# V's second pass with the weights' halves in spaced runs of 32 words

## What is computed

```python
u = u_emb[expert]
a = jax.nn.gelu(jnp.einsum('thkd,td->thk', u, xb), approximate=False)
coef = (g * a).astype(xb.dtype)
return jnp.einsum('thk,thkd->td', coef, v_emb[expert])
```

## Time and profile before

| | us |
|---|---|
| median of 3 runs (3255.95 to 3256.79) | 3256.68 |
| span of the profiled execution | 3254.9 |
| TensorE busy in it | 3242.3 |
| DVE busy | 2176.9 |
| ACT busy | 1675.9 |
| POOL busy | 119.5 |

### The profile page before, as it was taken

How to read it: one execution, slowest core, us unless ns; L and a number is a source line. 1 busy time by engine, 2 the same in 40 slices (tenths; PEclk the granted TensorE clock), 3 DMA queues, 4 the chain that set the end, 5 groups by cost and what they waited for, 6 DMA issues and landing times.

```text
span 3254.9 us, 60191 instructions
## 1 busy us (share of the span) xinstructions
PE 3242.3 (100%) x24752; PEld 3093.8 (95%) x24752; DVE 2176.9 (67%) x3677; ACT 1675.9 (51%) x2630; POOL 119.5 (4%) x157
## 2 busy tenths in 40 slices
PE   9999999999999999999999999999999999999998
PEld 9999999999999999999999999999999988888887
DVE  7987486666664487665765898878655555556655
ACT  5555554444444455544555444667544444455544
POOL 0001200000000100000000000222000000000000
PEclk9999999999999999999999999999999999999999
DMA  6444555555566656445656556444555555566554
GB/s 221 150 142 136 182 171 191 188 188 188 189 190 195 194 173 204 140 160 171 190 195 211 185 194 192 163 154 146 174 192 192 193 191 193 193 211 216 192 188 163
DMA packets 168801, 594.21 MB, mean 183 GB/s; under 512 B 19696, under 2 KB 21968, under 8 KB 168400
## 3 DMA queue, kind: packets, MB, share of 16 engines
q1 hardware_dynamic: 168528, 590.36, 55.4%
HBM read 584.55 MB, written 4.19 MB: 181 GB/s over the span
## 4 chain that ended last, share of the span: by engine, by line
PE 98%; DVE 1%; ACT 0%; DMA 0%; issue 0%; SPq 0%; DVEq 0%; ACTq 0%
PE ps L902 31%; PE ps L903 31%; PE ps L904 31%; PE ps L1344 2%; PE ps L957 0%; DVE wl L1437 0%; PE ps L909 0%; PE ps L929 0%; PE ps L1152 0%; DMA raw<-in_in1k 0%; PE ps L1175 0%; PE ps L1172 0%; PE ps L1358 0%; PE ps L1186 0%; PE ps L1176 0%; PE ps L1010 0%
## 5 line engine op out<-in xcount | busy, mean ns | idle before, releaser
L2201 ACT CAST wh<-raw 128x1024 fp32r<-128x1024 f32 (+2 forms) x1118 | 1159.9, 1038 | 1226.5 <-PE ps L904 1222.4
L1437 DVE TENSOR_TENSOR wl<-raw,wh 128x1024 fp32r<-128x1024 f32 (+2 forms) x1118 | 1347.9, 1207 | 502.1 <-ACT wh L2201 499.2
L902 PE MATMUL ps<-xh,wh 128*128 128x256 f32 x3088 | 863.2, 280 | 0.8 <-ACT vm L2494 0.7
L904 PE MATMUL ps<-xh,wl 128*128 128x256 f32 x3088 | 852.4, 276 | 0.0
L903 PE MATMUL ps<-xl,wh 128*128 128x256 f32 x3088 | 852.0, 276 | 0.0
L902 PE MATMUL ps<-xw,wh 128*128 128x260 f32 (+2 forms) x2096 | 595.4, 284 | 1.0 <-DVE wl L1437 0.9
L904 PE MATMUL ps<-xw,wl 128*128 128x260 f32 (+2 forms) x2096 | 590.3, 282 | 0.0
L902 PEld LDWEIGHTS ps<-xh,wh 128*128 128x128 f32 x3088 | 580.3, 188 | 5.3 <-ACT vm L2494 1.1
L903 PEld LDWEIGHTS ps<-xl,wh 128*128 128x128 f32 x3088 | 580.3, 188 | 1.6
L904 PEld LDWEIGHTS ps<-xh,wl 128*128 128x128 f32 x3088 | 579.8, 188 | 0.0
L903 PE MATMUL ps<-xw,wh 128*128 128x256 f32 (+2 forms) x1441 | 405.8, 282 | 0.0
(11 more groups left out here) (416 smaller groups left out, 4372.7 us busy)
## 6 DMA issues: line engine op xcount, KB each, us to landing
raw<-in_peer_u SPq DMA_DIRECT2D x256, 512.0 KB, 4.2
raw<-in_peer_v SPq DMA_DIRECT2D x256, 512.0 KB, 4.4
raw<-in_w_in SPq DMA_DIRECT2D x172, 512.0 KB, 3.7
raw<-in_w_up SPq DMA_DIRECT2D x82, 512.0 KB, 4.3
raw<-in_w_gate SPq DMA_DIRECT2D x80, 512.0 KB, 4.3
raw<-in_w_down SPq DMA_DIRECT2D x80, 512.0 KB, 4.1
raw<-in_w_out SPq DMA_DIRECT2D x64, 512.0 KB, 3.9
raw<-in_w_branch_a SPq DMA_DIRECT2D x16, 512.0 KB, 3.5
```

Of the source, the lines that this page charges most:

```text
L902: t.matmul(o, lh, rh, start=start, stop=False)
L904: return t.matmul(o, ll, rh, start=False, stop=stop)
L1437: v.tensor_tensor(part_at(wl, i), raw[:, i % RN, 0:cols(i)], part_at(wh, i).bitcast(F32), ALU.subtract).then_inc(lo, 1)
L2201: s.copy(part_at(wh, i), raw[:, i % RN, 0:cols(i)]).then_inc(hi, 1)
```

## The change

In the second pass of V the high and the low half of a chunk are no longer stored as 1024 contiguous words. A new array `comb` names the memory of `wh`, `wl`, `xh` and `xl` together (it begins at byte 23200 like `wh`). The function `V_part` gives a chunk's half in it: it begins 24 words (96 bytes) into `comb`, plus the slot's place, and so at a multiple of 256 bytes; of every 64 words (256 bytes) the second 32 are used (`side` 1). A half takes 8192 bytes of address and holds 4096. ACT's conversion and DVE's subtraction write it so (their count of words is the same), and the moving operand of a matmul is 16 runs of 32 words with a step of 256 bytes. Its output in PSUM stays 512 contiguous words. The three slots lie over `xh`, `xl` (two of them), and over `wh` and the front of `wl` (the third). `c_last` moves to word 4164 of `comb`, behind that third slot, and ACT's wait ahead of writing it is now for the whole first pass. All stages before the second pass, the waits of `cut`, the chunks and the order of the instructions on every engine stay as they are.

```diff
@@ -76,6 +76,7 @@
 RN, SN = 4, 3
 CH = 1024
+RUN = 32
@@ -503,6 +504,9 @@
     raw = alloc(top, "raw", [128, RN, CH])
+    comb_scope = ExitStack()
+    comb = alloc(comb_scope, "comb", [128, 2 * SN * (CH + 128) + 8832], F32R)
+    comb_scope.close()
     wh = alloc(top, "wh", [128, SN, CH + 128], F32R)
     wl = alloc(top, "wl", [128, SN, CH + 128], F32R)
@@ -613,7 +617,18 @@
-    c_last = [x[:, PAD_X[3] - 24:PAD_X[3] - 24 + S] for x in xbuf]
+    c_last = [comb[:, 4164 + S * n:4164 + S * n + S] for n in range(2)]
+
+    TOOTH = {V1 % SN: 6912, (V1 + 1) % SN: 6912 + 4 * CH, (V1 + 2) % SN: 0}
+
+    def V_part(w, i, half):
+        if i >= V1:
+            o = 24 + TOOTH[i % SN] + 2 * CH * half
+            return comb[:, o:o + 2 * CH].rearrange("p (b side k) -> p b side k", side=2, k=RUN)[:, :, 1, :]
+        return runs(w[:, i % SN, 0:CH])
+
+    def runs(a):
+        return a.rearrange("p (b k) -> p b k", k=RUN)
@@ -1374,9 +1389,9 @@
-            tk, dd = slice(128 * qt, 128 * qt + 128), slice(512 * b, 512 * b + 512)
-            return three(acc(half, qt, b)[:], coef_at(0, n)[:, tk], coef_at(1, n)[:, tk], wh[:, i % SN, dd], wl[:, i % SN, dd],
-                         j == 0, j == 127)
+            tk, dd = slice(128 * qt, 128 * qt + 128), slice(512 * b // RUN, (512 * b + 512) // RUN)
+            return three(runs(acc(half, qt, b)[:]), coef_at(0, n)[:, tk], coef_at(1, n)[:, tk], V_part(wh, i, 0)[:, dd],
+                         V_part(wl, i, 1)[:, dd], j == 0, j == 127)
@@ -1434,6 +1449,10 @@
             v.wait_ge(hi, i + 1)
+            if i >= V1:
+                v.tensor_tensor(V_part(wl, i, 1), runs(raw[:, i % RN, 0:CH]), V_part(wh, i, 0).bitcast(F32),
+                                ALU.subtract).then_inc(lo, 1)
+                return
@@ -2198,6 +2217,9 @@
                 s.wait_ge(gemm, i - SN + 1)
+            if i >= V1:
+                s.copy(V_part(wh, i, 0), runs(raw[:, i % RN, 0:CH])).then_inc(hi, 1)
+                return
@@ -2578,7 +2600,7 @@
             if n == 255:
-                s.wait_ge(gemm, AT["U", 127, 1] + 1)
+                s.wait_ge(gemm, V1)
```

## The result

The changed kernel takes 3263.19 us (median of 13 runs, 3262.61 to 3264.16), the kernel before 3256.68 in the same comparison: ratio 1.002, 95% interval 1.0013 to 1.0027. It is slower by 6.5 us, where 20.7 us less was forecast.

A forecast was written before the change was run, and what follows sets the result against it. TensorE's matmul count times start-to-start distance was taken to bound the kernel. Span 3254.9 - 22.2 (matmuls) + 1.5 (stalls) = 3234.2 us, plus 1.8 from span to median, gave 3236.0 us; range 3231 to 3262.

The forecast's parts named there:

- the two states: V's second pass: a matmul costs 544 cycles (226.7 ns) at first, 560 (233.3 ns) later, against 512 needed.
- Step 1: Second pass's 1536 matmuls: the moving operand in upper-half runs would take 216 ns each, 22.2 us less.
- the tax: Extra cycles of a float32r moving stream reading a 4-byte word every cycle: one in 16, 32 per 512 columns.
- three different places: Sign for a tax independent of address: streams beginning at three places in their 256 bytes all show 1 in 16.
- Steps 2 to 5: Second pass: conversion and subtraction cost the same, moved slots 0 us, moved last coefficients 1.5 us allowed, DMA 0 us.
- step 4: Last coefficients moved in `comb`: new wait 0 us; 1.5 us allowed for the end stall and `fin` steps with faster chunks.
- The second state: Second pass from about 3039 us: 560 cycles a matmul, begun where DVE's `fin` steps crowd its queue, never restored.
- Nothing changes: Rival for the second pass: unchanged mix, 3256.7 us, or second state throughout, 4.4 us more, 3261.1; chance 0.14.
- the tax stays: Rival for the second pass: tax remains, second state goes; all matmuls 226.7 ns, 5.8 us less, 3250.9; chance 0.16.
- The slower rival: Second pass: each jump over 128 unused bytes restarts the operand fetch; 576 cycles, 14.6 us more, 3271.3; chance 0.15.

The follow-up runs named there:

- e1_streams: Block replaced by a bench of TensorE matmuls alone, varying layouts of moving operand and weights: contiguous 544 to 560 cycles, runs of 32 in one half 564 to 576.
- e10_streams3: Third set of the TensorE-only bench, other spacings and weight places: alternating runs of 32 544 to 560 cycles, upper runs 564 to 576.
- e7_alt176: Changed kernel with runs of 32 words alternately in the lower and upper half of successive 256 bytes: 3255.54 us, ratio 0.9997 to the kernel before.
- e3_flat: Changed kernel with the same slots and waits, but each half of a chunk as 1024 contiguous words: 3256.12 us, ratio 0.9999 to the kernel before.
- e5_pad24: Kernel before with the coefficients (weights) moved by 16 bytes to the moving operand's place, 160 past a multiple of 256: 3251.42 us, ratio 0.9984.
- e4_streams2: TensorE-only bench, second set: runs of 32 words with steps of 96 or 160 words 544 cycles, steps of 64, 128 or 192 568.
- e8_alt0: e7_alt176 with the coefficients also beginning at a multiple of 256 bytes, as the runs do: 3262.13 us, ratio 1.0017 to the kernel before.

## Why the prediction was wrong

**What bounds the kernel: right.** The whole result is the pace of 1536 matmuls. The sum from the two states, and the reading that neither the clock nor another engine makes them, stand (e1_streams shows both without any other engine).

**Step 1 failed, in the value it took between its bounds.** The bounds, 213 and 240 ns, held the measured 235 ns. The value taken, 216, rested on reading "two extra cycles for each half of 256 bytes" as a toll for passing from one half to the other, which a stream in one half would not pay. The contiguous rows fit equally well a toll on each half entered, whichever half came before. The runs decide against the reading taken: the stream that never changes its half still pays the 32 cycles and more (564 to 576), which a toll on entering would explain, though not exactly (see e10_streams3). And going from one half to the same half of the next 256 bytes costs some 24 cycles more a matmul at the equal start (568 against 544) and 12 at the kernel's place of the weights (564 against e7_alt176's 552). The term was put at 216 ns a matmul and -22.2 us, and measured at 235 ns and +6.9 us. No row of the trace before had a gap or an address pattern that told the two apart; the half-rate passes of the earlier trace rows showed that the tax can vanish, not that halves are what makes it vanish. Two more readings were thinner than they look. "The pace is the same whether ACT and DVE work or idle" rested on one distance in the earlier trace rows; e1_streams is what shows it. And "three different places" were two in the rows (96 and 160 bytes); at the third, 16 bytes, the bench gives 272 to 288 cycles for 256 columns, by the place of the weights, so one cycle in 16 is the best case and no constant.

**Steps 2 to 5: right.** The conversion and the subtraction kept 1.05 and 1.23 us; the slots and the new wait cost nothing, as e3_flat shows; the stall at the end stayed at 0.7 us of weight load and 0.3 of TensorE, so the 1.5 us allowed in step 4 were not needed; TensorE waited for no DMA.

**The second state.** I took it for something that a disturbance starts. That is half of it. The disturbance chooses, but only because the weights begin 16 bytes behind the moving operand, where two paces are open; at 0 every burst and e5_pad24's whole pass had one.

**The rivals.** "Nothing changes" and "the tax stays" are the contiguous layout's story. The Trainium skill, "SBUF — State Buffer", "Who interferes with whom", lets the moving operand and the weight load go by independent ports without waiting; here the place of the weights alone moves a matmul between 544 and 560 cycles, so the measurement decides against it. The Trainium skill's note on 16-byte lines, on the same page under "Door 1: The DMA port swizzle", would have runs of 32 words stream as contiguous ones do; they do so only when they alternate (544), not in one half (568). The slower rival had the right side and a price too high, 3271.3 for 3263.2: it put 16 cycles on top of the second state, where 4 came. Its mechanism, a restart at each jump, is refuted by e4_streams2 (steps of 96 and 160 words are free).

**Open.** What in SBUF or in TensorE's reading makes the halves; why nothing goes below 544 (no layout tried did); why runs of 64 with a step of 96 pay 568; why runs that take 64 bytes of each half pay as much as runs in one half; the runs of 4 and 8 words; the better pace of wide weights. Weights kept in one half as runs were not tried; weights with one word in each 256 bytes cost 560 to 581 and say little.

## What to carry to other kernels

Where TensorE streams a 4-byte float32r operand in every cycle, look at the start-to-start distance and not at the busy time, and let the moving operand fill one half of 256 bytes and then the other in turn. Contiguous does it; gaps were free only where they were a multiple of 256 bytes, so that the next run begins, modulo 256, where the last one ended. Begin weights and moving operand at the same place within 256 bytes when matmuls have 512 columns: that one constant made this kernel 5.2 us quicker, and it costs no memory. But look at what else reads the same weights: in e8_alt0 the first pass lost more by their move than the second won. A regularity of contiguous streams says nothing on gapped ones: a bench of a few hundred matmuls per layout settled in one run what the trace could not.

## What the runs showed of the hardware

- Streams of 512 float32r columns: 544 cycles at best, 564 to 576 when all 128-byte runs lie in the same half of 256 bytes (weights contiguous, 128 columns), 555 to 581 with runs of 4 to 16 words, 1083 to 1088 when only one or two words in a row are used and as many skipped.
- Two stable paces, 544 and 560, for one and the same instruction stream at W - M = 16; in the kernel chunks 0.02 to 0.04 us late stood at the change from one to the other, which then held for over 800 matmuls.
- At 256 columns (M 16) the best places of the weights were W 80 and 160 with 272 cycles in all bursts, others 280 to 288 in most bursts; the equal start is not the best there (W 16: 280 to 284), as it was at 512 columns.
- The paces of the bench, without ACT, DVE or DMA beside it, are those of the kernel to the cycle: 544, 552, 560, 562, 564 and 568.
